# Row sums of modulation tiles 8 to 23: from one VectorE pass each to a GpSimd product and a ScalarE accumulation

## The reference

```python
c_act = jax.nn.silu(c)
mod = (c_act @ w_ada[l] + b_ada[l])[:, None, :]
shift1, scale1, gate1, shift2, scale2, gate2 = jnp.split(mod, N_MOD, axis=-1)
h = rms_norm(x, norm1_g[l]) * (1 + scale1) + shift1
proj = h @ w_in[l]
...
mixed = (g_attn * y_attn + g_pool * y_pool) @ w_out[l]
x = x + gate1 * mixed
h2 = rms_norm(x, norm2_g[l]) * (1 + scale2) + shift2
y_moe = hier_moe(h2, w_router_group[l], b_router_group[l], w_router_expert[l],
                 b_router_expert[l], w_expert_gate[l], w_expert_up[l], w_expert_down[l])
x = x + gate2 * y_moe
```

## Time and profile before

| | us |
|---|---|
| runs before, median of 3 | 1357.18 (1355.1 to 1358.43) |
| the profiled execution, as timed | 1355.56 |
| its span in the profile | 1353.8 |
| TensorE busy in the span | 1319.1 (97%) |
| VectorE busy | 657.1 (49%) |
| ScalarE busy | 292.6 (22%) |
| GpSimd busy | 7.8 (1%) |

### The profile page before, as it was taken

The page is one execution under the profiler, slowest core; times in us unless marked ns, Lnnn a source line. Parts: engine busy times, 40 slices in busy tenths (PEclk is TensorE's granted clock), DMA queues, the critical chain, the costliest instruction groups (busy, mean ns, idle before and its releaser), DMA issues.

```text
span 1353.8 us, 21296 instructions
## 1 busy us (share of the span) xinstructions
PE 1319.1 (97%) x8834; PEld 995.7 (74%) x8834; DVE 657.1 (49%) x1493; ACT 292.6 (22%) x601; POOL 7.8 (1%) x18
## 2 busy tenths in 40 slices
PE   8999999999999999888999999999999999999997
PEld 5999875443443443333688789999998878999997
DVE  6898464121001001000568647774546773867444
ACT  2223103111121121111343611210014261122000
POOL 0000000000000000000000000000000000000000
PEclk9999999999999999999999999999999999999999
DMA  9986996999999999999954054544444414544410
GB/s 389 404 367 245 416 420 246 421 414 421 421 422 420 423 421 422 423 421 420 392 201 141 32 186 156 180 164 166 177 156 142 156 47 156 176 167 163 181 63 32
DMA packets 52099, 364.63 MB, mean 269 GB/s; under 512 B 6161, under 2 KB 6465, under 8 KB 8994
## 3 DMA queue, kind: packets, MB, share of 16 engines
q1 hardware_dynamic: 49392, 355.49, 66.3%
q10 hardware_dynamic: 1890, 5.04, 1.2%
q0 software_dynamic: 720, 2.72, 0.5%
HBM read 359.02 MB, written 2.11 MB: 267 GB/s over the span
## 4 chain that ended last, share of the span: by engine, by line
PE 84%; DMA 11%; DVE 3%; issue 1%; ACT 0%; SPq 0%; DVEq 0%; ACTq 0%
PE bank L1222 31%; PE bank L923 19%; PE bank L667 15%; DMA ring<-in_weights 9%; PE bank L934 3%; PE bank L679 3%; DMA ringx<-in_weights 2%; PE bank L1367 2%; PE bank L1138 2%; PE bank L757 1%; PE bank L908 1%; PE bank L1271 1%; DVE ring L1847 1%; PE bank L1322 1%; PE bank L1348 1%
## 5 line engine op out<-in xcount | busy, mean ns | idle before, releaser
L923 PE MATMUL bank<-ring,cst 128*64 128x512 f32 x600 | 167.6, 595 | 6.9 <-DMA ring<-in_weights 5.5
L1222 PE MATMUL bank<-h,ring 128*128 128x128 f32 x1056 | 134.8, 276 | 1.1 <-DVE gate L2469 0.6
L667 PE MATMUL bank<-h,ring 128*128 128x256 f32 x576 | 129.2, 384 | 3.1 <-issue 2.1
L1222 PEld LDWEIGHTS bank<-h,ring 128*128 128x128 f32 x1056 | 126.1, 192 | 2.5 <-issue 2.4
L2169 DVE TENSOR_TENSOR act<-act,bank 128x512 f32<-128x512 f32 (+1 forms) x17 | 11.1, 656 | 239.9 <-PE bank L923 239.9
L667 PEld LDWEIGHTS bank<-h,ring 128*128 128x128 f32 x576 | 109.4, 191 | 20.1 <-issue 2.9
L923 PEld LDWEIGHTS bank<-ring,cst 128*64 128x64 f32 x600 | 52.6, 137 | 91.2 <-issue 89.4
L1222 PE MATMUL bank<-hid,ring 128*128 128x128 f32 x912 | 115.6, 275 | 0.0
L1222 PEld LDWEIGHTS bank<-hid,ring 128*128 128x128 f32 x912 | 108.6, 192 | 0.0
L1222 PE MATMUL bank<-sq,ring 128*128 128x128 f32 x720 | 95.1, 275 | 0.0
L923 PE MATMUL bank<-ringx,cst 128*64 128x512 f32 x256 | 90.3, 595 | 4.0 <-DMA ring<-in_weights 2.1
(11 more groups left out here) (425 smaller groups left out, 1932.8 us busy)
## 6 DMA issues: line engine op xcount, KB each, us to landing
ring<-in_weights SPq DMA_DIRECT2D x251, 1024.0 KB, 10.1
ringx<-in_weights SPq DMA_DIRECT2D x44, 1024.0 KB, 22.8
spare<-in_weights SPq DMA_DIRECT2D x18, 1024.0 KB, 21.2
pool_a<-in_weights SPq DMA_DIRECT2D x9, 1024.0 KB, 23.0
x<-in_weights SPq DMA_DIRECT2D x9, 1024.0 KB, 22.4
ring<-in_weights SPq DMA_DIRECT2D x6, 512.0 KB, 19.6
x<-in_x SPq DMA_DIRECT2D x1, 1024.0 KB, 5.0
pool_a<-in_cst ACTq DMA_DIRECT2D x1, 1024.0 KB, 19.9
```

The costliest lines, as they stand in the source:

```text
L667: ins = e.matmul(u.ap[:, 0:S], w[:, k * width + j * P:k * width + (j + 1) * P], acts[:, k, :], start=k == 0, stop=k == kc - 1)
L923: ins = e.matmul(g.bank[bank][ex * SLOTS:(ex + 1) * SLOTS, :], stat(m, ex), pair[ex][:, m * 512:(m + 1) * 512], start=first and m == 0, st ...
L1222: ins = e.matmul(u.ap[:, at * P:(at + 1) * P], stat[:, k, :], moving[:, k, :], start=k == 0 and (of == 1 or (b == 0 and first)), stop=k == ...
```

## The change

Tiles 8 to 23 leave VectorE. GpSimd multiplies each block by the row of silu(c) in place (`pool_ada`), ScalarE runs over the product with an Identity activation that accumulates along the row (`act_ada`), and VectorE adds the bias to eight columns of `g.mod` at a time (`dve_biased`), four times. `modulated` is now raised by ScalarE for these tiles. GpSimd does tile 8 between writing the bias rows and loading them back, the others behind those loads and ahead of the slot constants. ScalarE has the passes between its own steps: tile 8 before the first copy for v, 9 to 11 after the next three copies, 12 to 16 after the steps of gates 0, 2, 3, 5 and 6, 17 to 21 before the squares of the output, 22 and 23 after squares 0 and 2. In `LOADS`, b3 and modulation tiles 19 to 21 move ahead of some expert tiles; the slots stay the same.

```diff
@@ -148,7 +148,7 @@
 RF = 11
 FSEVENS = 12
 LOADS = ("a4 a0 i0 a5 a1 i1 i2 a6 a2 a7 a3 i3 i4 i5 i6 a8 i7 a9 i8 a10 i9 a11 i10 i11 e e e e i12 a12 e i13 a13 i14 a14 i15 a15 b0 a16 "
-         "e15 b1 a17 a18 b2 e11 e20 e21 b3 e17 e14 a19 b4 a20 b5 a21 b6 a22 b7 a23 e18 e12 e13 e e e e e16 e e e19").split()
+         "e15 b1 a17 a18 b2 b3 e11 a19 e20 e21 b4 a20 e17 b5 a21 e14 b6 a22 b7 a23 e18 e12 e13 e e e e e16 e e e19").split()
 RELEASED = ("a4 a0 a5 a1 a6 a2 a7 a3 i0 i1 i2 i3 a8 i4 a9 i5 a10 i6 a11 i7 i8 i9 a12 i10 i11 a13 i12 a14 a15 i13 a16 i14 i15 a17 b0 a18 "
             "b1 a19 b2 a20 b3 a21 a22 b4 a23 b5 b6 b7").split()
 FIRST_ORDER = [n for n in LOADS if n[0] != "e"]
@@ -213,7 +213,7 @@
 
 SLOT, USE, BEFORE = slots()
 
-SEMS = ("x_in prm_in prm_late memory_set cst_in late_in tab_in pool_in row_out bias_in mask_in slots_in result_out slots_freed modulated "
+SEMS = ("x_in prm_in prm_late memory_set cst_in late_in tab_in pool_in row_out bias_in mask_in slots_in result_out slots_freed modulated multiplied "
         "c_in gated scale_ready squares sq_added recip root h_scaled h_shifted trig_ready rope_ready lb_diff lb_exp "
         "dve_step shift_routed rms_ready route_exp_in route_exp_out picked summed x_placed starts_ready most_known x_moe xw x_out "
         "row_exp prob mixed1 "
@@ -1454,6 +1454,7 @@
     for oc in range(8):
         ps = g.full(e, "qk", oc)
         g.read(("qk", oc), e.copy((g.q3 if oc < 4 else g.k3)[:, oc % 4, :], ps[:, 0:S]))
+    act_ada(e, g, 8)
     act_first_product(e, g, ("vu", 0), g.first_a)
     r, r2 = g.pbuf[2], g.pbuf[3]
     e.wait_ge(s["trig_ready"], 1)
@@ -1465,6 +1466,7 @@
     for j in range(1, 4):
         g.evac(e, "vu", j - 1, 0)
         act_first_product(e, g, ("vu", j), g.first_a)
+        act_ada(e, g, 8 + j)
     act_attention_step(e, g, A, 0)
     e.wait_ge(s["row_out"], 16)
     e.wait_ge(s["prm_late"], 16)
@@ -1473,6 +1475,8 @@
         act_first_product(e, g, ("gate", j), g.first_a)
         if j < 5:
             act_attention_step(e, g, A, j + 1)
+        if j in (0, 2, 3, 5, 6):
+            act_ada(e, g, 12 + (0, 2, 3, 5, 6).index(j))
         for n in range(j) if j == 5 else (j - 1,) if j > 5 else ():
             act_gate(e, g, n)
     act_gate(e, g, 7)
@@ -1484,9 +1488,13 @@
         ps = g.full(e, "pol", gr)
         g.read(("pol", gr), e.mul(g.pol[:, gr, :], ps[:, 0:S], g.p("pool_scale", gr, 1)))
     e.activation(g.small[:, 44:45], g.c("ones", 0, 1), ACT.Sqrt)
+    for n in range(17, 22):
+        act_ada(e, g, n)
     for k in range(KC):
         g.evac(e, "out", k)
         e.activation(g.sq[:, k, :], g.x[:, k, :], ACT.Square).then_inc(s["squares"], 1)
+        if k in (0, 2):
+            act_ada(e, g, 22 + k // 2)
     g.evac(e, "ss", 1)
     e.activation(g.rms, g.rms, ACT.Sqrt).then_inc(s["root"], 1)
 
@@ -1849,6 +1857,31 @@
     ins.then_inc(g.s["modulated"], 1)
 
 
+def dve_biased(e, g, n):
+
+    modulated(e, g, n + 3)
+    of = g.mod[:, 2 * n:2 * n + 8]
+    g.step.up(e.tensor_tensor(of, of, g.p("b_ada", 2 * n, 8), ALU.add))
+
+
+def pool_ada(e, g, n):
+
+    w = g.filled(e, ada_tile(n))
+    v = w[:, :].rearrange("p (b d) -> p b d", b=2)
+    for block in range(2):
+        e.tensor_tensor(v[:, block, :], v[:, block, :], g.cact, ALU.mult).then_inc(g.s["multiplied"], 1)
+
+
+def act_ada(e, g, n):
+
+    w = g.ring[SLOT[ada_tile(n)]]
+    for block in range(2):
+        e.wait_ge(g.s["multiplied"], 2 * (n - 8) + block + 1)
+        o = w[:, block * D:(block + 1) * D]
+        ins = e.activation(o, o, ACT.Identity, accum_out=g.mod[:, 2 * n + block:2 * n + block + 1])
+    ins.then_inc(g.s["modulated"], 1)
+
+
 def dve_normed(e, g, m):
 
     e.wait_ge(g.s["root"], 1)
@@ -1886,7 +1919,6 @@
     dve_first_sums(e, g, 1)
     dve_angles(e, g)
     for j in range(4):
-        dve_ada(e, g, 8 + j)
         dve_tokens_seven(e, g, j)
         dve_first_sums(e, g, j + 2)
     dve_scores(e, g, A, 0)
@@ -1898,40 +1930,37 @@
             dve_first_sums(e, g, 6 + j)
         if j == 4:
             dve_bounds(e, g)
-        if j in (1, 3, 4, 5):
-            dve_ada(e, g, (12, 13, 14, 15)[(1, 3, 4, 5).index(j)])
-        if j == 6:
-            modulated(e, g, 15)
+        if j == 7:
+            dve_biased(e, g, 8)
+            dve_biased(e, g, 12)
+            g.after(e)
             e.tensor_tensor(g.shift_parts.rearrange("p (k r) -> p k r", k=KC), g.p("w_router").rearrange("p (k r) -> p k r", k=KC),
                             g.mod[:, 24:32].unsqueeze(2).to_broadcast([P, KC, 36]), ALU.mult).then_inc(s["shift_routed"], 1)
-            dve_ada(e, g, 16)
             e.wait_ge(s["shift_routed"], 1)
             e.tensor_reduce(g.shift_sum, g.shift_parts.rearrange("p (k r) -> p r k", k=KC), AX.X, ALU.add).then_inc(s["shift_routed"], 1)
 
     mixed = g.h
     e.wait_ge(s["gated"], 16)
     for oc in range(KC):
-        if oc % 3 == 0:
-            if oc == 0:
-                ps = g.full(e, "zb")
-                g.read(("zb",), e.tensor_tensor(g.zb, ps[:, 0:36], g.p("b_router"), ALU.add))
-            dve_ada(e, g, 17 + oc // 3)
+        if oc == 0:
+            ps = g.full(e, "zb")
+            g.read(("zb",), e.tensor_tensor(g.zb, ps[:, 0:36], g.p("b_router"), ALU.add))
         ps = g.full(e, "attn", oc)
         g.read(("attn", oc), e.tensor_tensor(mixed[:, oc, :], g.gate3[:, oc, :], ps[:, 0:S], ALU.mult))
     for oc in range(KC):
-        if oc in (2, 6):
-            dve_ada(e, g, 20 + oc // 4)
+        if oc == 4:
+            dve_biased(e, g, 16)
+            g.after(e)
+            step.up(e.scalar_tensor_tensor(out=g.sc2[:, :], in0=g.mod[:, 32:40], scalar=1.0, in1=g.p("g2"), op0=ALU.add, op1=ALU.mult))
+            sc2_done = step.n
         ps = g.full(e, "pool", oc)
         g.read(("pool", oc), e.tensor_tensor(g.gate3[:, 8 + oc, :], g.gate3[:, 8 + oc, :], ps[:, 0:S], ALU.mult))
         g.evac(e, "pool", oc)
         g.evac(e, "attn", oc)
         e.tensor_tensor(mixed[:, oc, :], mixed[:, oc, :], g.gate3[:, 8 + oc, :], ALU.add).then_inc(s["mixed1"], 1)
-    modulated(e, g, 19)
-    step.up(e.scalar_tensor_tensor(out=g.sc2[:, :], in0=g.mod[:, 32:40], scalar=1.0, in1=g.p("g2"), op0=ALU.add, op1=ALU.mult))
-    sc2_done = step.n
     for oc in range(KC):
-        if oc in (0, 2):
-            dve_ada(e, g, 22 + oc // 2)
+        if oc == 6:
+            dve_biased(e, g, 20)
         if oc > 1:
             dve_add_squares(e, g, 1, oc - 1, 1, g.sq)
         ps = g.full(e, "out", oc)
@@ -2627,12 +2656,17 @@
     g.evac(e, "row")
     e.wait_ge(s["h_shifted"], BIAS_AFTER)
     e.dma_start(g.dram["row"], g.row[0:HEADS, :]).then_inc(s["row_out"], 16)
+    g.evac(e, "c", 0)
+    g.evac(e, "c", 1)
+    pool_ada(e, g, 8)
     e.wait_ge(s["row_out"], 16)
     for qt in range(ST):
         nk = (qt + 1) * P
         src = bass.AP(g.dram["row"].tensor, 0, [[1, P], [NB_ROW, HEADS], [1, nk]])
         o = 0 if qt == 0 else HEADS * P
         e.dma_start(g.bias[:, o:o + HEADS * nk].rearrange("p (h k) -> p h k", h=HEADS), src).then_inc(s["bias_in"], 16)
+    for n in range(9, T_ADA):
+        pool_ada(e, g, n)
     e.wait_ge(s["bias_in"], 32)
     g.full(e, "pol", 3)
     e.dma_start(g.slot_cst[:, :], g.dram["slots"]).then_inc(s["slots_in"], 16)
```

## The result

The changed kernel takes **1372.39 us** (median of 4 runs, 1369.86 to 1376.82) beside 1356.85 for the kernel before on the same chip: ratio 1.0121, 95% interval 1.0108 to 1.0134. It is 15.5 us slower, outside the forecast's range. The profiled execution is the run of 1376.82 us (span 1374.7), 4.4 above the median; its stalls are read from it, and sums of the whole are made of medians.

The account below looks back on a forecast made before the run. TensorE's path up to the experts was taken as the bound, with a full weight stream after it. 6.8 − 0.5 − 5.1 + 4.4 = +5.6 us gave 1362.8 us on the median; whole range 1356.0 to 1368.5.

Parts of the forecast that it names:

- GpSimd beside VectorE: Half sums at gates 0 to 2 and a late mixing add wait for GpSimd products: +4.4 us, bounds 0 and 7.9.
- the clock's term: TensorE's clock may fall after the new hold at tile 12: taken as 0, at most 1.7 us.
- tile 12's hold: Tile 12's ScalarE pass delays gate 1's copy to 97.4, so gate 2's block starts 6.8 us late.
- 2.4 us (tile 13, gates 1 and 2): Tile 13's products meet the half sums of gates 1 and 2: 2.4 us taken, up to 4.7.
- The 0.5 us at 102.78: TensorE's one wait seen on VectorE before the output stage, 0.50 us, would go.
- The output stage, −5.1: Late row sums of tiles 19 and 20 no longer hold TensorE in the output stage: 5.1 us gained.
- The durations: At 1024 columns, GpSimd's product takes 2.35 us; ScalarE's accumulating pass 1.09 us, 1.27 with readout.
- free passing: Rival 1: VectorE and GpSimd pass each other freely, +1.2 us, 1358.4; chance 0.36.
- rival 2: GpSimd is held after issuing the second bias load until it lands at 77.7: +6.0 us, 1363.2; chance 0.08.
- rival 3: The hold at tile 12 does not reach TensorE at gate 2's block: −5.6 us, 1351.6; chance 0.06.
- rival 4: Sums of tiles 19 to 21 come no sooner, output stage keeps its holes: +6.3 us, 1363.5; chance 0.04.
- sign of being wrong: First expert reload before 223 us, or gate 1's copy before 95, meaning products at half the price.

Follow-up runs that it names:

- the kernel with the early loads: Changed kernel with both bias loads issued ahead of tiles 9 to 11's products, GpSimd then waiting for the second v tile's copy step: 1367.78 us.
- the one with the wait: Changed kernel with GpSimd waiting, after the second bias load's issue, for four sets of half sums before tiles 9 to 11's products: 1366.39 us.
- the issue last: The changed kernel with GpSimd's wait for four sets of half sums, the second bias load issued behind it, directly ahead of the six products: 1370.02 us.
- with gaps: Changed kernel with GpSimd waiting for ScalarE's pass over the tile before, ahead of tiles 10 and 11: 1367.28 us.
- the short product: Changed kernel with tile 9's first product cut into 4 and 1020 columns, a short instruction between load issue and long products: 1370.86 us.
- with copies: Changed kernel with GpSimd's products replaced by copies of each block onto itself: 3376.26 us, with the branch for overflowing experts running.
- the old loads: Changed kernel with the order of loads of the kernel before: 1377.25 us.

## Why the prediction was wrong, point by point

**The step that failed is "GpSimd beside VectorE", priced at +4.4 us with bounds 0 and 7.9.** It measured some 14.8: 18.1 for the products' length, less the 3.3 that belong to the step on tile 12 (up to 5.1 us of it are products that run slowly behind the stalls, the clock's term below). The bounds were built on one premise: a VectorE operation waits at most for one product. The nearest row showed no wait at all, and one product was taken as the other end; no row of the kernel before had a run of products behind a load's issue. There the wait is the whole run. The run itself was foreseen (from 65.6 us; it began at 64.50), but only the half sums of gate 0 were set against it. The set before, for the second u tile, stands at 63.7 in both kernels; it was left out, and it is the one that was held. The trace of the changed kernel shows 15.20 us where the premise allowed 2.35 more than 0.69. The Trainium skill, "SBUF — State Buffer", section "Who interferes with whom", has the later of two operations wait until the first is through; the half sums of 2.7 to 2.9 us agree, the one of 15.20 does not, and the measurement decides.

Still, the long hold is not most of the loss. The runs that make it into turns (1366.39, 1367.78 and 1367.28 us) win 4.6 to 6.0 us of the 18.1. The larger part is plain turn-taking, which the step also put too low, in two places. Up to gate 2: in the kernel with the early loads six half sums lose 0.7 to 2.2 us each, and TensorE stands 3.04 us for the first set; in the one with the wait it stands 5.56 for gate 0's. I took the half sums of gate 0 to lie under tile 12's hold and left 0.8 of them. In the three runs that break up the long hold, gate 2's block is 7.4 to 9.2 us late, 1.3 to 3.1 more than with tile 12's hold alone.

And from gate 2 to the branches I counted 2.4 us (tile 13, gates 1 and 2). The run with tiles 8 to 11 on VectorE shows (168.81 − 155.99) − 6.1 = 6.7, and the changed kernel 24.5 − 14.6 = 9.9. In the former 1.3 net is slow products right behind tile 12's hold, and tile 13 holds nothing on the path. Beside tiles 15 and 16 half sums of gate 6 (2.84 us each) and two steps of four columns (2.2 to 2.3) are held, so that gate 7's half sums come late and TensorE stands 3.52 us; the shift's sum ahead of L800 costs another 1.16. In the changed kernel tile 14 meets the half sums of gate 4 as well, and the bias adds, which I had put into VectorE's idle time at nothing, are held too: a pair of 8 columns each took 2.32 us, and TensorE stood 3.30 for the sum behind it.

**Tile 12's hold, +6.8**: 6.1 where it can be seen alone. Right in place and size, and covered in the changed kernel by the larger stall. The 0.5 us at 102.78 went as forecast: from gate 2's block to gate 3's it is 8.9 us, before 9.5. It was not the only wait on VectorE before the output stage, as the prediction has it: 0.59 us stood ahead of gate 1's block at 84.42, and 1.03 do so in the changed kernel.

**The output stage, −5.1**: the profiled run gains (24.5 − 20.1) = 4.4 by the start of the last routing products (224.67 against 204.56); 0.72 us of idle time remains, behind a mixing add that waited for a product. The reason holds too, measured against TensorE's path. Tile 19's load goes out at 170.8 instead of 143.3, as its slot hangs on ScalarE's pass, but lands in 4.8 us, 4.8 ahead of the start of the branch products; before, it landed 7.4 behind that start (163.37 against 155.99). On the kernel before, the new loads alone give 3.6 us, so most of this term needed no GpSimd.

**The durations** were right: GpSimd's product 2.31 undisturbed (2.416 mean with turns; forecast 2.35), ScalarE's pass 1055 ns and its readout 189 (1.09 us and 186 ns). The two groups, from the page and from the groups of ScalarE by form (busy us, mean ns of one, idle time before):

```profile
L1872 POOL TENSOR_TENSOR ring<-ring,c_row 128x1024 f32<-128x1024 f32 x32 | 76.5, 2416 | 83.9 <-DMA ring<-in_weights 83.9
...
L1881 ACT ACTIVATE ring<-ring 128x1024 f32<-128x1024 f32 x32 | 33.7, 1055 | 36.3 <-POOL ring L1872 36.3
L1881 ACT ACTIVATION_READ_ACCUMULATOR ring<-ring 128x1 f32 x32 | 6.1, 189 | 0.0
```

**The clock, 0**, was wrong: after the long stall 24 products took 2.0 us more, after the one ahead of 127.94 another 1.5, and after the one ahead of 162.93 eight products 1.6 (3.55 at 163.14; 1.97 in the kernel before). The forecast had 1.7 as the end for one fall, at tile 12's hold. With products of 4 columns that hold stands alone, and the 32 products behind it at 96.06 took 1.6 us more, with a grant of 0.50, that is 1.2 GHz, from 96.0 to 98.5: the end of the range, not the 0.

Of the rivals, free passing would have been 1358.4; the kernel with products of 4 columns, 1354.3, shows what that meant at best. GpSimd was not held behind the second bias load (rival 2): the first product starts at 64.50, where the issue ends. Tile 12's hold did reach TensorE (rival 3), and the output stage lost its holes but 0.72 us (rival 4). Neither sign of being wrong showed, the reload before 223 or gate 1's copy before 95: they came at 245.01 and 104.74. Both were set against a loss forecast too high, and it was forecast too low.

## What to carry to other kernels

Work moved to an idle engine is not free when both engines work in SBUF: here 76 us of GpSimd products cost the SBUF-only operations of VectorE that met them up to one product of waiting each, and TensorE waited with them wherever VectorE had no slack. Before such a move, list which operations of the other engine read from PSUM (here they passed) and which do not, and where those stand on the path; and do not start a run of GpSimd work straight behind a load that GpSimd issues, but let GpSimd stand in a wait between. Shorter instructions may help as well: copies of 1.0 us cost 1.2 us up to the experts over products of 4 columns. But whole products cut into short pieces were not run. Here the gain that the move aimed at was to be had from the order of loads and of one row sum, without a second engine.

## What was unexpected of the hardware

- Six times (the changed kernel, and the runs with the issue last, with gaps, with the short product, with copies and with the old loads) a run of GpSimd operations stood directly behind a load's issue, and each time one VectorE operation was held to the run's end: 15.20, 6.83, 5.68, 14.51, 3.47 and 14.98 us. Beside runs that began behind a wait in which GpSimd stood, no half sum took over 2.9 us in any kernel. Why the issue makes the difference is not shown; only that it does, that a wait in which GpSimd stands (1.1 us was enough) ends it, and that a short product or a wait already met does not.
- Some VectorE operations with a single tensor operand in SBUF are held as well: a conversion of 256 columns took 2.45 us at 48.91 beside tile 8's products, 0.29 without. Others are not: reciprocals of one column never took over 0.17 us beside a product. Small size alone does not help: two-operand steps of four columns took 2.2 to 2.3 us. Operations that read one operand from PSUM were never held: in all these traces none of them took over 0.49 us beside a product.
